# Storing the attention bias's shifted rows from between the chunks of the first MLP instead of at the kernel's beginning

## What is computed

```python
def first_block(x, ...):
    h = rms_norm(x, norm_mix_g[l])
    u = h @ w_in[l]
    u_pool, q_raw, f_raw, i_raw, g_raw = jnp.split(u, splits, axis=-1)
    y_pool = pool_mixer(u_pool, pool_w[l], pool_scale[l])
    y_hgrn = hgrn2_mixer(q_raw, f_raw, i_raw, g_raw, lower_bounds[l], hgrn_norm_g[l])
    x = x + jnp.concatenate([y_pool, y_hgrn], axis=-1) @ w_out[l]
    h2 = rms_norm(x, norm_mlp_g[l])
    x = x + jnp.square(jax.nn.relu(h2 @ w_up[l])) @ w_down[l]        # the first MLP
    return rms_norm(x, final_norm_g)

def _neighbourhood_attention(q, k, v, rpb):                          # second block
    ...
    col_off = jnp.clip(kc - q_col[..., None] + NA_KW - 1, 0, 2 * NA_KW - 2)
    rpb_col = rpb.astype(jnp.float32)[:, :, col_off]
    ...
        bias = jnp.take(rpb_col, row_off, axis=1).transpose(0, 2, 3, 1, 4)
        sc = jnp.einsum("bnqhd,bknjhd->bhnqkj", q_r, k_r).astype(jnp.float32) * scale
        sc = jnp.where(mask, sc + bias[None], NEG)
```

## Time and profile before

| | |
|---|---|
| time, median of 3 executions | 2798.74 us (2798.08 to 2799.75) |
| span of the profiled execution | 2796.3 us |
| PE busy | 2665.6 us (95% of the span) |
| DVE busy | 1457.1 us (52%) |
| POOL busy | 913.8 us (33%) |
| ACT busy | 643.2 us (23%) |

### The profile page before, as it was taken

The page is one execution under the profiler, slowest core; times in us unless marked ns, Lnnn a source line. Parts: engine busy times, 40 slices in busy tenths (PEclk is TensorE's granted clock), DMA queues, the critical chain, the costliest instruction groups (busy, mean ns, idle before and its releaser), DMA issues.

```text
span 2796.3 us, 33903 instructions
## 1 busy us (share of the span) xinstructions
PE 2665.6 (95%) x12569; PEld 2197.9 (79%) x12569; DVE 1457.1 (52%) x1657; ACT 643.2 (23%) x844; POOL 913.8 (33%) x481
## 2 busy tenths in 40 slices
PE   8399999999999999999898889999999999999997
PEld 7288887878888888887776667888878888888886
DVE  7245555443343443437888887223155555555555
ACT  4133333230110101114244445001131111111113
POOL 2012222233333333333443343323333333333333
PEclk9699999999999999999999999999999999999999
DMA  5111111212111111111310011112211111111111
GB/s 198 18 31 30 37 30 38 83 57 61 48 45 53 45 53 45 45 53 45 107 35 22 23 36 31 52 47 68 90 46 45 53 45 45 53 45 51 47 45 75
DMA packets 201585, 144.96 MB, mean 52 GB/s; under 512 B 14095, under 2 KB 183738, under 8 KB 200506
## 3 DMA queue, kind: packets, MB, share of 16 engines
q1 hardware_dynamic: 189604, 122.92, 14.3%
q10 hardware_dynamic: 11926, 21.28, 2.3%
HBM read 131.59 MB, written 14.36 MB: 52 GB/s over the span
## 4 chain that ended last, share of the span: by engine, by line
PE 78%; DVE 14%; issue 4%; ACTq 2%; ACT 2%; DVEq 1%; DMA 0%; SPq 0%
PE psum L681 50%; PE psum L700 16%; DVE conv_t L2030 4%; PE psum L1085 3%; PE psum L804 2%; ACTq L1273 2%; DVE h_lo L1673 1%; PE psum L720 1%; PE psum L1002 1%; DVE ffn_gate L2206 1%; DVE prob L2096 1%; DVE x_t L1927 1%; PE psum L1185 1%; PE psum L1019 1%; DVE sq_sum L1668 1%
## 5 line engine op out<-in xcount | busy, mean ns | idle before, releaser
L620 POOL CAST w_hi<-w_raw 128x1024 fp32r<-128x1024 f32 x212 | 239.5, 1130 | 1665.9 <-issue 836.3
L681 PE MATMUL psum<-h_hi,w_hi 128*128 128x512 f32 x2384 | 755.1, 396 | 9.9 <-DVE h_lo L1776 5.4
L681 PE MATMUL psum<-h_lo,w_hi 128*128 128x512 f32 x2384 | 743.5, 391 | 0.0
L681 PE MATMUL psum<-h_hi,w_lo 128*128 128x512 f32 x2384 | 741.8, 390 | 0.0
L622 POOL TENSOR_TENSOR w_lo<-w_raw,w_hi 128x1024 fp32r<-128x1024 f32 x212 | 569.4, 2686 | 17.0
L681 PEld LDWEIGHTS psum<-h_hi,w_hi 128*128 128x128 f32 x2384 | 444.3, 189 | 107.8 <-issue 15.3
L681 PEld LDWEIGHTS psum<-h_lo,w_hi 128*128 128x128 f32 x2384 | 449.6, 189 | 94.8
L681 PEld LDWEIGHTS psum<-h_hi,w_lo 128*128 128x128 f32 x2384 | 449.4, 188 | 95.0
L1927 DVE TENSOR_TENSOR x_t<-x_t,psum 128x512 f32<-128x512 f32 x416 | 281.6, 684 | 194.9 <-PE psum L700 192.8
L2198 DVE TENSOR_TENSOR ffn_z<-psum,rinv 128x1024 f32<-128x1024 f32 x44 | 53.9, 1224 | 272.9 <-PE psum L681 267.3
L700 PE MATMUL psum<-mlp_lo,w_hi 128*128 128x512 f32 x480 | 186.8, 389 | 0.0
(11 more groups left out here) (284 smaller groups left out, 2954.9 us busy)
## 6 DMA issues: line engine op xcount, KB each, us to landing
w_raw<-in_w_up SPq DMA_DIRECT2D x152, 256.0 KB, 3.1
w_raw<-in_w_in SPq DMA_DIRECT2D x124, 256.0 KB, 3.1
w_raw<-in_w_down SPq DMA_DIRECT2D x108, 256.0 KB, 2.8
w_raw<-in_w_out SPq DMA_DIRECT2D x32, 256.0 KB, 3.1
x_in<-in_x SPq DMA_DIRECT2D x8, 512.0 KB, 8.2
x_spill<-x_t ACTq DMA_DIRECT2D x1, 4096.0 KB, 12.3
x_spill<-x_t ACTq DMA_DIRECT2D x4, 1024.0 KB, 4.6
x_t<-x_spill ACTq DMA_DIRECT2D x1, 4096.0 KB, 12.3
```

The lines of the kernel that those rows point to most:

```text
L620: pool.tensor_copy(hi, w_raw[:, slot, :]).then_inc(weight_hi, 1)
L681: last = pe.matmul(psum[:, first_bank + t, :], w, a[:, k, t * HALF:(t + 1) * HALF], start=(k == 0 and j == 0), stop=(k == KT - 1 and j == 2))
```

## The change

The 8 transfers that fill `shifted` are taken out of the first stage. The one of head 0 is issued behind chunk 0 of the first MLP, and that of head h+1 behind chunk h+1, with the 3 transfers of head h that read `shifted` just ahead of it. These 3 now wait for the `shifted` of their own head instead of all eight. For this ACT's first 8 turns of its MLP loop are written out; the other engines' programs stay as they are.

```diff
             act.dma_start(pair_mask[:, :], dram["c_pair_mask"]).then_inc(pool_loaded, 16)
 
 
-            act.wait_ge(rpb_stored, 16 * 3)
-            for h in range(NA_HEADS):
-                by_distance = bass.AP(rpb_rows.tensor, h * RPB_H * RPB_W + SHIFTS - 1,
-                                      [[RPB_W, SHIFT_ROWS], [-1, SHIFTS], [1, GROUP_W]])
-                act.dma_start(shifted[h, :, :, :].rearrange("i r c -> r i c"), by_distance).then_inc(shifted_stored, 16)
-
             act.wait_ge(cols_turned, 1)
             act.activation(cols[:, :], psum[:, 2, :], ACT.Copy).then_inc(cols_ready, 1)
...
             split_activations(mlp_a, mlp_hi, 0, None)
 
 
-            act.wait_ge(shifted_stored, 16 * NA_HEADS)
-            step = SHIFT_ROWS * GROUP_W
-            for h in range(NA_HEADS):
+            def store_shifted(h):
+
+                act.wait_ge(rpb_stored, 16 * 3)
+                by_distance = bass.AP(rpb_rows.tensor, h * RPB_H * RPB_W + SHIFTS - 1,
+                                      [[RPB_W, SHIFT_ROWS], [-1, SHIFTS], [1, GROUP_W]])
+                act.dma_start(shifted[h, :, :, :].rearrange("i r c -> r i c"), by_distance).then_inc(shifted_stored, 16)
+
+            def store_near(h):
+
+                act.wait_ge(shifted_stored, 16 * (h + 1))
+                step = SHIFT_ROWS * GROUP_W
                 for m in range(3):
                     near = bass.AP(shifted.tensor, ((h + 1) * SHIFTS - GROUP_W * (m + 1)) * step + (ROWS - 1) * GROUP_W,
                                    [[step, GROUP_W], [-GROUP_W, ROWS], [1, P]])
                     act.dma_start(bias_rows[h // 2, :, h % 2, m, :].rearrange("(r c) k -> c r k", c=GROUP_W), near)\
                        .then_inc(bias_stored, 16)
-            with act.Fori(0, MLP_CHUNKS - 2) as i:
+
+            def mlp_chunk(i):
                 mlp_square(i + 1)
                 split_activations(mlp_a, mlp_hi, i * 2 + 2, i * 4 + (T_MLP + 6))
+
+            store_shifted(0)
+            for h in range(NA_HEADS):
+                mlp_chunk(h)
+                store_near(h)
+                if h + 1 < NA_HEADS:
+                    store_shifted(h + 1)
+            with act.Fori(NA_HEADS, MLP_CHUNKS - 2) as i:
+                mlp_chunk(i)
             mlp_square(MLP_CHUNKS - 1)
             split_activations(mlp_a, mlp_hi_last, 2 * MLP_CHUNKS - 2, None)
```

## The result

| | before | changed |
|---|---|---|
| median | 2799.24 us (2798.08 to 2799.84, 4 runs) | 2748.01 us (2747.37 to 2751.05, 4 runs) |
| span of the profiled execution | 2796.3 us | 2745.6 us |

The ratio is 0.9819, with a 95% interval of 0.9805 to 0.9833: the changed kernel is faster by 1.8%, 51.2 us.

What follows compares the result with a forecast made beforehand. PE, busy 95% of the span, was taken as the bound, with one 46.9 us wait for ACT's copy to `cols`. 46.45 + 1.9 = 48.3 us off 2798.7 gave 2750.4 us, range 2748.5 to 2754.

Steps and rivals of the forecast that it cites:

- L904 begins at 79.78: Pooling branch's small product on PE: waits last for `zq`, starts at 79.78 instead of 126.23, saving 46.45 us.
- The clock: First half of L904: with only 0.4 us idle ahead, PE runs it at full clock, saving 1.9 us more, bounds 0 to 1.9.
- The removed issues were the cause: First stage: ACT's 63.6 us of `shifted` issues ahead of `cols` delay L904, so removing them frees PE.
- An issue alone costs 0.70: ACT in the MLP: one `shifted` issue per chunk of 43.52 us, taken as 0.70 us, at most 9.50.
- The MLP covers it: MLP chunks: ACT, held 2.7 us and at most 11.7 per chunk, delays PE by 0 us.
- The cover of about 55 us: MLP: PE loses nothing until ACT is held for about 55 us in a chunk.
- Weight loads beside `shifted`: MLP weight loads sharing DMA engines with `shifted`: land within 6.1 us, 11 us before their split, cost 0.
- Two rules of the Trainium skill: Issues are usually short beside transfers (would give 5.6 us, 2793.1); engines divide the slowest dimension, one for 31 rows.
- Behind it everything only moves: From the head stage to the end: PE, DVE and ACT keep their order, the rest shifts unchanged, cost 0.

Runs made afterwards that it cites:

- the runs with gaps of 12.0 and 23.5 us: Changed kernel with four `shifted` issues at the old place, 2762.92 us; kernel before with each `shifted` transfer cut into 17 and 14 rows, 2778.16 us.
- the run with two: Changed kernel with the `shifted` transfers of heads 0 and 1 issued at the old place, the other six in the MLP: 2750.12 us.

## Why the prediction was right, step by step

- **L904 begins at 79.78: 46.45 us.** It began at 79.99, which is 46.24; the stage ahead of it ran 0.2 us later. `zq` was the last to come, as said.
- **The clock, 1.9 us.** 5.80 − 3.69 = 2.1. Together the head stage begins 48.35 us earlier, at 85.15, the figure given; that it fits to the hundredth is luck, since two errors of 0.2 us cancel. That the clock belongs to the gap is shown by the runs with gaps of 12.0 and 23.5 us, where L904 took 6.70 and 5.96; in the six profiles without a gap it took 3.69. A longer gap doesn't cost more: 5.80 behind 46.9 us.
- **The removed issues were the cause.** Shown from both sides: 2 at the old place cost nothing that could be told apart, 4 cost what the chain says, and cutting them at their place gave the whole gain.
- **An issue alone costs 0.70, of bounds 0.70 to 9.50.** It is 0.60 in the MLP. The reason given, an idle queue behind the first issue, was a misreading: `pair_mask` was still on its way. Not that a transfer stands ahead, but how long and of what shape it is, makes the hold.
- **The MLP covers it, 0 us.** PE's downward piece of chunk 0 began at 638.56 before and at 590.17 after, 48.39 earlier. The last upward one stood at 1226.08 before and stands at 1177.69 after, again 48.39 (the changed kernel's pieces are below). The cover of about 55 us measured 57.

```profile
590.17 21.76 PE psum L700 x96
...
1177.69 21.76 PE psum L681 x96
```

- **Weight loads beside `shifted`: 0 us.** From 606 to 960 us in the changed kernel they landed in 2.7 to 5.6 us, against 2.6 to 4.6 before. So some came up to 1 us later, but POOL's waits over the MLP are the same as before, none above 7.4 us.
- **Two rules of the Trainium skill, both on its page "DMA: Bandwidth & Descriptors".** That a sequencer's issue is usually small beside the transfer (section "Issuing engines are not separate DMA queues") does not hold for these issues when they stand behind one another (8.7 us), and holds when one stands alone (0.60 us). The rule on the number of engines, used only as a bound in the prediction, fits the 8.7, the cuts and the packet counts.
- **The term that was mis-sized: "Behind it everything only moves", cost 0.** The spans differ by 50.7 us and not 48.35. The chain shows where the 2.35 us come in: 0.04 by the MLP, 0.6 in the attention pairs, and 1.6 in the last matmuls of L700, in the second MLP's last turn.

The last of these: the piece in the chain and the stretch around it (clock as last but two number), first of the kernel before, then of the changed one. PE waited 3.4 us ahead of it in both.

```profile
2741.50 8.71 PE psum L700 x30
...
2741.40:2751.00 9.60, 9.50 (x35) 7.67 (x36) 5.28 (x9) 0.00 (x0) 1.67 (x1) 0.82 0.00 0
```

```profile
2692.43 7.09 PE psum L700 x30
...
2692.40:2700.30 7.90, 7.87 (x35) 6.52 (x36) 5.16 (x8) 0.00 (x0) 1.62 (x1) 1.00 0.00 0
```

The same 30 matmuls after the same wait ran at a granted clock of 0.82 before and at 1.00 after. The attention pairs show it too: a stretch of some 85 us for each of the four pairs at 0.96, 0.96, 0.94 and 0.94 before, all at 0.96 after. The change touches neither place. But in the nine profiles this piece took 7.1 us in the five kernels that reach it by 2707 us, and 8.7 to 9.7 us in the four that reach it from 2720 us on. The medians lean the same way: the run with 17 and 14 rows, whose head stage begins 26.8 us after the changed kernel's, is 30.2 us slower. So the time at which the kernel gets there may decide, and then these 2.35 us belong to what the change gives; with one profile of each kernel, chance isn't ruled out. The cause stays open. It is also the whole distance between forecast and median, 2.4 us.

## What to carry to other kernels

An engine that issues transfers can be held by a transfer ahead of them, here by one whose slowest dimension was 31 or 17: look for issues that take as long as their transfer, and ask what stands behind them on that engine. Then there are two remedies: shorten the transfer (here a slowest dimension of 31 rows cut into 16 and 15 gave everything, in place), or put single issues where the engine can be spared for longer than one lasts. For the second, the cover must be read at the new place, as the idle time up to the next thing that the bound engine really wants; 57 us in one MLP chunk was plenty for 2.6 us and too little for 91, and the first head had some 7 us.

## What was not expected

- With the same number of runs the shape decides: a head's transfer in one piece of 31 rows held ACT for 8.7 us, in 16 and 15 rows for twice 0.75, in 17 and 14 rows for 5.3 together.
- The second transfer of a row is held, and the first is not: 0.70 and 9.03 us in the run with two.
- A lower clock of PE shows up after some waits of only 1.9 us and not after others: L709 at 50 us, which no edit touches, took 1.95 to 1.97 us in five of the nine profiles and 2.44 to 3.40 in four. The piece at the tail, behind 3.4 us, does the like. Each is worth 1 to 3 us of the time, about as much as executions of one kernel differ by.
